# A three-branch transformer block and a two-layer block: the side work of the first three branches set out anew

## The chip, the cores and the metric

One Trainium2 chip, one of its cores. The metric is the device time of one execution in microseconds (us). Before the change the median of 3 runs is 2276.05 us (2275.41 to 2276.76).

## What the reference computes

512 tokens of width 1024 go through a first block with three mixers side by side and then through a second block of two layers. The change touches the three mixers of the first block alone.

```
h = rmsnorm(x);  proj = h @ w_in      # q,k,v of A; q,f,i,g of B; c_q,c_kv,c_kr of C; gate logits
y_a = chunked_relpos_attention(a_q, a_k, a_v, rel_bias)     # 8 heads of 64, softmax
y_b = hgrn2_recurrence(b_q, b_f, b_i, b_g, ...)             # q -> silu(q); k = sigmoid(-f)
                                                            # gated by silu(g)
y_c = mla_attention(c_q, c_kv, c_kr, ...)                   # rmsnorm of c_q and c_kv first
merged = sum over n of sigmoid(gate_n) * (y_n @ w_branch[n])
x = x + merged @ w_out;  x = x + relu(h2 @ w_ff1)^2 @ w_ff2
```

All is in 32-bit floats. Each dense product is made of three matmuls with operands split in a high part (rounded to the fp32r type) and a low part: high by low, high by high, low by high.

## The kernel before, in words

A planner (class `Plan`) writes one list of steps. Each engine's program walks the same list in order and emits its own part of a step, so the list sets the order on every engine, and each engine runs its queue strictly in that order. Semaphores carry the dependences. Nothing is reordered on the chip by due time or cost.

The dense products are the backbone. A "unit" is one weight tile's product. A `rows` unit has 128 output columns and eight 128-deep steps; it is issued in four pieces of six matmuls. A `cols` unit has 512 columns for four token blocks, in 16 pieces of six matmuls, and takes its weights in four chunks. Weights come by DMA into two buffers `raw`; ACT copies a chunk to its high part (`split`, L1321) and DVE makes the low part in the following piece (`split_low`, through `low`, L1642). The last piece of a unit or chunk is followed by the split of the chunk two further on, and by the step `ev`, which empties the unit's PSUM bank.

With some units a "side" generator is interleaved: `interleave(main, side, ratio)` places `ratio` side ticks behind each dense piece on average, so now and then two in a row. Beside the units `uB` (query and output-gate inputs of mixer B, 8 units, 32 pieces) runs attention A, 39 ticks; beside `uGA` (gates and projection of A, 48 pieces) runs the recurrence of B; beside `uGB` runs mixer C (`mla`). Between them stand `uF` (the values, then the forget gates of B; one `cols` unit each) and `uC` (latents of C).

In a tick n of attention A, PE computes scores n and n+1 (even n, L1009), transposes the weights of item n-4 into bank 6 (L910), and DVE adds the bias, takes the maximum of item n-1 and normalises item n-2. ACT exponentiates item n-1 (L1445), then copies the transposed item n-4 out of bank 6 (`turned`, L1462). Bank 6 is the only bank for these transposes, so the transpose of one item waits for the copy of the item before.

A logistic 1/(1+exp(-z)) is three ACT instructions on a 128x512 tile: Exp, Ln, Exp (L1417, L1419, L1421), each waiting for the one before. For `bq`, `bg` and `gate` units they stand back to back in `ev`, after DVE has scaled the bank (`scale`, L1757). For `bq` and `bg` the step `ev2`, one piece later, lets DVE multiply the bank by the logistic (L1860, L1862) and so frees the bank (2 or 3, in turn).

The forget gates (`bf`) are four steps of DVE and ACT on four token blocks (L1873, L1880, L1883 on DVE; L1428, L1430, L1434 on ACT), after which PE turns the keys (`h_turn`). The latent norm is one step `c_norm`: ACT squares four blocks and takes their roots, then DVE scales them in eight instructions (L2046, L2047); PE turns them in `c_turn`.

Of the kernel before, what the change touches and what calls it, by code (L numbers as in the profile page):

```python
# [8 lines left out]
ACT = mybir.ActivationFunctionType  # L9
# [158 lines left out]
def cols(w, c0, ncol, src, ev, **arg):  # L168
    return Unit("cols", w, 0, 8, c0, ncol, src, ev, **arg)
# [84 lines left out]
class Plan:  # L254
# [57 lines left out]
    def ready(self, u, j):  # L312

        steps = (self.split(u.chunks[0] + 2) if j == u.n - 1 else []) + [("ev", u, j)]
        if u.ev == "out" and u.arg["norm"] is not None:
            self.defer(1, "ev_low", u, j)
        if u.ev == "up" and u.arg["n"] == 2:
            self.defer(2 if u.arg["m"] < 4 else 1000, "merge", u.arg["m"] + j)
        if u.arg.get("ship"):
            self.defer(2, "ship", u, j)  # L320
        if u.ev in ("bq", "bg"):
            self.defer(1, "ev2", u)
        return steps

    def heads(self, u):
# [60 lines left out]

    def hgrn(self):

        for _ in range(7):
            yield []  # L390
        for p in range(4):
            yield [("h_turn", p)]
        for tt in range(4):
            yield [("h_decay", tt)]
        exps = [(p, lv) for p in range(4) for lv in (1, 2, 3, 7, 4, 5, 6)]
        ends = []
        yield [("h_zero",), ("h_exp", *exps.pop(0))]
        yield [("h_weigh", 0, 1), ("h_exp", *exps.pop(0))]
        weigh = [(0, 2)]
        for p in range(4):  # L400
            for lv in range(8):
                tick = [("h_weigh", *w) for w in weigh]
                weigh = []
                if ends:
                    tick.append(ends.pop(0))
                if lv < 7:
                    tick.append(("h_score", p, lv))
                    if lv == 2:
                        tick.append(("h_state", p))
# [12 lines left out]

    def mla(self):

        def steps(g):
            return [[(n, g, i)] for n in ("c_q", "c_kv", "c_qt", "c_kt") for i in range(4)]

        for _ in range(7):
            yield []
        for j in range(3):  # L430
            yield [("c_turn", j)]
        yield [("c_rope",)]
        yield from steps(0)
# [20 lines left out]
    def make(self):  # L454
        win, win2a, win2b = ("w_in", 0), ("w_in_2", 0), ("w_in_2", 1)
        h0, h1 = ("h", 0), ("merged", 1)
# [2 lines left out]
        uA += [cols(win, 1024, 512, h0, "vcopy", to="F3")]  # L459
        uB = [rows(win, 0, 8, 1536 + j * P, P, h0, "bq", j=j, wk=4 + j) for j in range(4)]  # L460
        uB += [rows(win, 0, 8, 3072 + j * P, P, h0, "bg", j=j, wk=4 + j) for j in range(4)]
        uF = [cols(win, 2560, 512, h0, "vcopy", to="F0"), cols(win, 2048, 512, h0, "bf")]
        uGA = self.gate_up(0, "yA")
        uC = [cols(win, 3584, 416, h0, "c")]
        uGB = self.gate_up(1, "yB")
# [71 lines left out]
        self.banks = (0, 1, 6, 7)  # L537
        self.run(self.dense(uA[8:]))
        self.banks = (2, 3)
        self.run(interleave(self.dense(uB), self.attn(ATTN["A"]), 39 / 32))  # L540
        uF[0].banks, uF[1].banks = [0, 1, 4, 5], [2, 3, 6, 7]
        self.run(self.dense(uF))
        self.banks = (0, 1)
        recurrence = list(self.hgrn())
        self.run(interleave(self.dense(uGA, {i: [("bf", uF[1], i)] for i in range(4)}), iter(recurrence[:-4]), 49 / 48, False))
        self.banks = (0, 1, 4, 5)
        self.run(self.dense(uC, {2 + 2 * i: t for i, t in enumerate(recurrence[-4:])}))
        self.add("c_norm")
# [348 lines left out]
def tensor_program(pe, S, B, plan):  # L897
# [226 lines left out]
    def h_state(p):  # L1124
        two = [empty(b) for b in h_pair(p, 7)]
        at.wait_ge("hg_dk", 4)
        for tt in range(4):
            at.wait_ge(*plan.freed(plan.uF[0], tt)[0])
        k4, v4 = B.f4("F1"), B.f4("F0")
        for c in range(7):  # L1130
            rr, cs = slice(64 * (c % 2), 64 * (c % 2) + 64), slice((c // 2) * 64, (c // 2) * 64 + 64)
            for hf in range(2):
                hs = slice(p * P + 64 * hf, p * P + 64 * hf + 64)
                last = pe.matmul(two[c % 2][64 * hf:64 * hf + 64, cs], k4[rr, c // 2, hs], v4[rr, c // 2, hs],
                                 start=c < 2, stop=True, skip_group_check=True)
# [162 lines left out]
def scalar_program(act, S, B, plan, load_table):  # L1298
# [106 lines left out]
    def sigmoid(u):  # L1405
        bank = B.bank[u.banks[0]]
        if u.ev == "gate":
            w = B.W[u.arg["at"] % 4]
            bank = w
        else:  # L1410
            w = B.W[u.arg["wk"]]
            if "before" in u.arg:
                at.wait_ge("ev_d", u.arg["before"].dve[0])
                if u.ev == "fgate":
                    at.wait_ge("f_lo", u.arg["before"].arg["tile"] + 1)
        at.wait_ge("ev_s", u.scaled[0])
        act.activation(w[:], bank[:], ACT.Exp, scale=-1.0).then_inc(S["ev_a"], 1)  # L1417
        at.wait_ge("ev_a", u.act[0])
        act.activation(w[:], w[:], ACT.Ln, bias=one).then_inc(S["sig"], 1)  # L1419
        at.wait_ge("sig", u.sig - 1)  # L1420
        act.activation(w[:], w[:], ACT.Exp, scale=-1.0).then_inc(S["sig"], 1)  # L1421

    def bf(u, i):
        k = B.f4("F1")
# [10 lines left out]


    def attn(a, n):
        i = n - a.e
        if 0 <= i < a.nt:
            nk, w, st = (a.where(i)[1] + 1) * P, B.W[a.P1[i % 4]], B.stat(i)  # L1440
            src = w if a.name == "A" else B.bank[a.X[i % len(a.X)]]
            if i >= 4:
                at.wait_ge("at_t", a.i(i - 4))
            at.wait_ge("at_m", a.i(i))
            act.activation(w[:, 0:nk], src[:, 0:nk], ACT.Exp, bias=st[:, 0:1],  # L1445
                           accum_out=st[:, 1:2]).then_inc(S["at_e"], 1)
        if 0 <= n - a.t < a.nt:
            turned(a, n - a.t)
        p = a.ends(n - a.o - 1)
        if p is not None:  # L1450
            y = a.pair(p) - 1
            ys = slice(y % 4 * T, (y % 4 + 1) * T)
            at.wait_ge("at_o", y + 1)
            act.copy(B.R[0][:, ys], B.bank[7][:]).then_inc(S["at_yh"], 1)
# [80 lines left out]
        act.copy(B.R[2][:, p * T:(p + 1) * T], B.V(3)).then_inc(S["yb_h"], 1)  # L1535


    def c_norm():
        at.wait_ge("hg_s", 28)
        for tt in range(4):  # L1540
            o, w, s = B.c_tokens()[:, tt, :], B.W[4 + tt], B.stat(tt)
            at.wait_ge(*plan.freed(plan.uC[0], tt)[0])
            act.activation(w[:, 0:256], o[:, 0:256], ACT.Square, accum_out=s[:, 0:1]).then_inc(S["c_n"], 1)
            act.activation(w[:, 256:384], o[:, 256:384], ACT.Square, accum_out=s[:, 1:2]).then_inc(S["c_n"], 1)
        s = B.st[:, 0:32].rearrange("p (t c) -> p t c", t=4)
        at.wait_ge("c_n", 8)
        act.activation(s[:, :, 2:3], s[:, :, 0:1], ACT.Ln, bias=eps, scale=1.0 / 256).then_inc(S["c_n"], 1)
        act.activation(s[:, :, 3:4], s[:, :, 1:2], ACT.Ln, bias=eps, scale=1.0 / 128).then_inc(S["c_n"], 1)
        at.wait_ge("c_n", 10)
        act.activation(s[:, :, 2:4], s[:, :, 2:4], ACT.Exp, scale=-0.5).then_inc(S["c_n"], 1)  # L1550
# [67 lines left out]
    def dt(u, h):  # L1618
# [3 lines left out]
        act.mul(B.F[u.arg["to"]][:, h * T:(h + 1) * T], B.bank[6][:], gain).then_inc(S["dt_a"], 1)  # L1622

    todo = {"begin": begin, "late": late, "split": split, "first": first, "root": root, "root2": root2, "merge": merge, "at": attn, "df": diff, "df_soft": diff_soft, "df_norm": diff_norm,
            "ev": ev, "ev_low": ev_low, "bf": bf,
            "h_decay": h_decay, "h_exp": h_exp, "h_sq": h_sq, "h_ms": h_ms, "h_low": h_low, "c_norm": c_norm, "c_q": c_q,
            "c_qt": c_qt, "c_kv": c_kv, "c_kt": c_kt, "sb": sb, "dn_sq": dn_sq, "dn_root": dn_root, "dt": dt}
    for step in plan.steps:
        if step[0] in todo:
# [6 lines left out]
def vector_program(dve, S, B, plan):  # L1636
# [402 lines left out]
        low(B.R[3][:, ps], B.V(3), B.R[2][:, ps], "yb_l")  # L2039


    def c_norm():
        for tt in range(4):
            o, s = B.F["F4"][:, tt * 416:(tt + 1) * 416], B.stat(tt)
            at.wait_ge("c_n", 11)
            dve.tensor_scalar(o[:, 0:256], o[:, 0:256], s[:, 2:3], None, ALU.mult).then_inc(S["c_u"], 1)  # L2046
# [406 lines left out]
```

## Time and profile before

| | value |
|---|---|
| median of 3 runs | 2276.05 us |
| the profiled execution | 2277.32 us, span 2275.6 us |
| granted TensorE clock, mean | 0.996 of full speed |
| PE busy | 2220.9 us (98%) |
| DVE, ACT, POOL busy | 1200.1, 940.3, 219.6 us |
| chain of waits, shares | PE 89%, DVE 4%, ACT 4%, issue 2% |

PE's busy time leaves 54.7 us of the span. The page's 40 slices show where: PE stands at 8 tenths in the first slice and at 9 in all others. Where an idle time of PE is shown in the timeline, the engine named behind the arrow is the one whose instruction ended it.

### The profile page before, as it was taken

Reading aid. Unit: us, or ns where it says so; the run is one execution under the profiler, and the core shown is the slowest. Engines: PE = TensorE matmul, PEld = TensorE weight load, DVE = VectorE, ACT = ScalarE, POOL = GpSimd, SP = SyncE. Lnnn points to the kernel's source line nnn. Section 1 sums busy time; section 2 is a strip of 40 time slices with the busy share of each in tenths; the row PEclk is TensorE's granted clock in tenths of the full one; section 3 lists DMA queues with packets and bytes.
Section 4 is the critical chain, followed back from the end, with each engine's and each line's share of the span. In section 5 each row is a group of like instructions: output and inputs, shape, how many; then the busy total and the mean of one; then the engine's idle time right before and its main releaser. Section 6 shows DMA issues by size and latency. Waiting matters only on the chain.

```text
span 2275.6 us, 26925 instructions
## 1 busy us (share of the span) xinstructions
PE 2220.9 (98%) x10484; PEld 1733.9 (76%) x10484; DVE 1200.1 (53%) x1827; ACT 940.3 (41%) x1561; POOL 219.6 (10%) x312
## 2 busy tenths in 40 slices
PE   8989999999999999999999999999999999999999
PEld 6658788667888888877565788888887657888887
DVE  4573664555544444473445555545545685555454
ACT  4463433455443223243545533333435565333331
POOL 0000121211210000030323200000120001000000
PEclk9999999999999999999999999999999999999999
DMA  5212111212323222322011232222321112332233
GB/s 171 74 42 88 47 37 63 68 38 102 102 93 100 96 96 98 102 84 93 29 56 38 74 102 93 95 100 93 102 93 65 56 47 68 101 101 92 93 102 102
DMA packets 52111, 187.48 MB, mean 82 GB/s; under 512 B 5905, under 2 KB 6033, under 8 KB 51857
## 3 DMA queue, kind: packets, MB, share of 16 engines
q1 hardware_dynamic: 51984, 185.76, 24.6%
q8 instruction: 84, 1.38, 0.3%
q14 instruction: 43, 0.34, 0.1%
HBM read 183.64 MB, written 2.10 MB: 82 GB/s over the span
## 4 chain that ended last, share of the span: by engine, by line
PE 89%; DVE 4%; ACT 4%; issue 2%; POOL 1%; DMA 1%; SPq 0%; ACTq 0%; DVEq 0%; POOLq 0%
PE ps L925 22%; PE ps L928 21%; PE ps L926 21%; PE ps L946 4%; PE ps L949 3%; PE ps L947 3%; PE ps L1269 2%; PE ps L910 2%; PE ps L1120 1%; PE ps L1153 1%; PE ps L1257 1%; PE ps L1245 1%; ACT wh L1321 1%; PE ps L1273 1%; PE ps L1033 1%
## 5 line engine op out<-in xcount | busy, mean ns | idle before, releaser
L1321 ACT CAST wh<-raw 128x1024 fp32r<-128x1024 f32 (+1 forms) x336 | 353.0, 1051 | 874.1 <-PE ps L928 758.3
L925 PE MATMUL ps<-hh,wl 128*128 128x512 f32 x1408 | 566.9, 403 | 14.6 <-DVE wl L1642 13.2
L928 PE MATMUL ps<-hl,wh 128*128 128x512 f32 x1408 | 551.2, 391 | 0.0
L926 PE MATMUL ps<-hh,wh 128*128 128x512 f32 x1408 | 550.4, 391 | 0.0
L1642 DVE TENSOR_TENSOR wl<-raw,wh 128x1024 fp32r<-128x1024 f32 (+1 forms) x336 | 416.4, 1239 | 191.5 <-ACT wh L1321 190.4
L925 PE MATMUL ps<-R,wl 128*128 128x512 f32 x896 | 359.5, 401 | 7.3 <-issue 5.8
L928 PE MATMUL ps<-R,wh 128*128 128x512 f32 x896 | 350.6, 391 | 0.0
L926 PE MATMUL ps<-R,wh 128*128 128x512 f32 x896 | 350.1, 391 | 0.0
L925 PEld LDWEIGHTS ps<-hh,wl 128*128 128x128 f32 x1408 | 265.7, 189 | 73.3 <-issue 20.4
L928 PEld LDWEIGHTS ps<-hl,wh 128*128 128x128 f32 x1408 | 265.4, 188 | 56.9 <-DVE hl L1721 0.3
L926 PEld LDWEIGHTS ps<-hh,wh 128*128 128x128 f32 x1408 | 265.8, 189 | 55.9 <-issue 2.9
L1852 DVE TENSOR_TENSOR x<-ps,x 128x512 f32<-128x512 f32 x192 | 131.6, 689 | 143.2 <-PE ps L928 143.2
L925 PEld LDWEIGHTS ps<-R,wl 128*128 128x128 f32 x896 | 169.1, 189 | 46.6 <-issue 11.1
L928 PEld LDWEIGHTS ps<-R,wh 128*128 128x128 f32 x896 | 168.9, 188 | 36.2 <-DVE R L1642 0.4
L926 PEld LDWEIGHTS ps<-R,wh 128*128 128x128 f32 x896 | 168.9, 189 | 35.2 <-issue 1.4
L946 PE MATMUL ps<-wh,hh 128*128 128x512 f32 (+1 forms) x384 | 155.4, 405 | 1.0 <-ACT F L1376 0.5
L949 PE MATMUL ps<-wh,hl 128*128 128x512 f32 (+1 forms) x384 | 148.9, 388 | 0.0
L947 PE MATMUL ps<-wl,hh 128*128 128x512 f32 (+1 forms) x384 | 148.7, 387 | 0.0
L2161 POOL TENSOR_TENSOR W<-W 128x512 f32<-128x512 f32 x30 | 48.6, 1620 | 837.8 <-ACT W L1340 837.1
L1757 DVE TENSOR_TENSOR ps<-ps,W 128x512 f32<-128x512 f32 x96 | 67.2, 700 | 114.3 <-PE ps L928 114.3
L1642 DVE TENSOR_TENSOR R<-W,R 128x512 fp32r<-128x512 f32 x84 | 58.2, 693 | 87.4 <-ACT R L1403 78.7
L946 PEld LDWEIGHTS ps<-wh,hh 128*128 128x128 f32 x384 | 72.3, 188 | 23.7 <-issue 9.7
(225 smaller groups left out, 2195.5 us busy)
## 6 DMA issues: line engine op xcount, KB each, us to landing
raw<-in_weights SPq DMA_DIRECT2D x332, 512.0 KB, 3.3
x<-in_x_t SPq DMA_DIRECT2D x4, 512.0 KB, 7.2
F<-in_x_t SPq DMA_DIRECT2D x4, 512.0 KB, 4.6
out<-x SPq DMA_DIRECT2D x8, 256.0 KB, 2.1
raw<-in_weights SPq DMA_DIRECT2D x4, 416.0 KB, 3.1
x<-in_bias SPq DMA_DIRECT2D x1, 1024.0 KB, 6.2
C<-in_consts SPq DMA_DIRECT2D x1, 832.0 KB, 6.8
F<-in_weights SPq DMA_DIRECT2D x2, 384.0 KB, 3.6
```

The source lines that it names most:

```text
L910: last = pe.transpose(bank[0:rows, i * P:(i + 1) * P], a, ident)
L925: pe.matmul(out, lo[:, k, cs], xh, start=k == 0, stop=False)
L926: pe.matmul(out, hi[:, k, cs], xh, start=False, stop=False)
L928: last = pe.matmul(out, hi[:, k, cs], xl, start=False, stop=k == u.nk - 1)
L946: pe.matmul(out, B.hh[:, ts], hi[:, kk, :], start=k == 0, stop=False)
L947: pe.matmul(out, B.hh[:, ts], lo[:, kk, :], start=False, stop=False)
L949: last = pe.matmul(out, B.hl[:, ts], hi[:, kk, :], start=False, stop=k == 7)
L1321: act.copy(B.wh[s][:, 0:nk * ncol], B.raw[s][:, 0:nk * ncol]).then_inc(S["w_hi"], 1)
L1642: dve.tensor_tensor(lo, src, hi.bitcast(F32), ALU.subtract).then_inc(S[name], 1)
L1757: dve.tensor_tensor(to[:], B.bank[u.banks[j]][:], B.W[8][:], ALU.mult).then_inc(S["ev_s"], 1)
L1852: dve.tensor_tensor(B.xt(m), bank[:], before, ALU.add).then_inc(S["ev_d"], 1)
L2161: pool.tensor_tensor(B.W[0][:], B.W[0][:], B.W[m][:], ALU.add).then_inc(S["n_addp"], 1)
```

## The change

Five things are moved; no arithmetic is added or left out.

- In attention A ACT's copy `turned` stands ahead of the exponential of the same tick.
- The second and third instruction of a logistic become steps of their own (`sig2`, `sig3`), one and two pieces after `ev`, for `bq`, `bg` and `gate`; `ev2` stands three pieces after instead of one. For the feed-forward gates (`fgate`) the three stay together.
- The unit of the forget gates comes ahead of the values. Attention A's 39 ticks are spread over 36 pieces (32 of `uB`, 4 of the forget gates) instead of 32. The four `bf` steps stand beside the values' pieces instead of `uGA`'s first ones.
- The recurrence begins after 2 empty ticks instead of 7, with 44 ticks to 48 pieces instead of 49.
- The latent norm's DVE scalings become two side ticks and its ACT part five, inside `mla`, in place of seven empty ticks.

```diff
@@ ready
+        if u.ev in ("bq", "bg", "gate"):
+            self.defer(1, "sig2", u)
+            self.defer(2, "sig3", u)
         if u.ev in ("bq", "bg"):
-            self.defer(1, "ev2", u)
+            self.defer(3, "ev2", u)
@@ hgrn
-        for _ in range(7):
+        for _ in range(2):
             yield []
@@ mla
-        for _ in range(7):
-            yield []
+        for tt in range(4):
+            yield [("c_sq", tt)]
+        yield [("c_root",)]
+        for i in range(2):
+            yield [("c_norm", i)]
@@ make
-        uF = [cols(win, 2560, 512, h0, "vcopy", to="F0"), cols(win, 2048, 512, h0, "bf")]
+        uF = [cols(win, 2048, 512, h0, "bf"), cols(win, 2560, 512, h0, "vcopy", to="F0")]
...
-        self.run(interleave(self.dense(uB), self.attn(ATTN["A"]), 39 / 32))
         uF[0].banks, uF[1].banks = [0, 1, 4, 5], [2, 3, 6, 7]
-        self.run(self.dense(uF))
+        made = list(self.dense(uB + uF, {49 + 3 * i: [("bf", uF[0], i)] for i in range(4)}))
+        self.run(interleave(iter(made[:36]), self.attn(ATTN["A"]), 39 / 36))
+        self.run(made[36:])
...
-        self.run(interleave(self.dense(uGA, {i: [("bf", uF[1], i)] for i in range(4)}), iter(recurrence[:-4]), 49 / 48, False))
+        self.run(interleave(self.dense(uGA), iter(recurrence[:-4]), 44 / 48, False))
...
-        self.add("c_norm")
@@ scalar_program: sigmoid
         act.activation(w[:], bank[:], ACT.Exp, scale=-1.0).then_inc(S["ev_a"], 1)
+        if u.ev == "fgate":
+            sig2(u)
+            sig3(u)
+    def sig2(u):
         at.wait_ge("ev_a", u.act[0])
-        act.activation(w[:], w[:], ACT.Ln, bias=one).then_inc(S["sig"], 1)
+        act.activation(sig_tile(u)[:], sig_tile(u)[:], ACT.Ln, bias=one).then_inc(S["sig"], 1)
+    def sig3(u):
         at.wait_ge("sig", u.sig - 1)
-        act.activation(w[:], w[:], ACT.Exp, scale=-1.0).then_inc(S["sig"], 1)
+        act.activation(sig_tile(u)[:], sig_tile(u)[:], ACT.Exp, scale=-1.0).then_inc(S["sig"], 1)
@@ scalar_program: attn
+        if a.name == "A" and 0 <= n - a.t < a.nt:
+            turned(a, n - a.t)
         i = n - a.e
...
-        if 0 <= n - a.t < a.nt:
+        if a.name != "A" and 0 <= n - a.t < a.nt:
             turned(a, n - a.t)
```

ACT's queue in attention A, around the second `bq` unit: W5 is that unit's logistic, W0 to W3 the attention items, F7, F5, F8 the transposed items' places, wh the high weights. Before:

```order
L1462 COPY F7<-ps 128x3x128
L1321 CAST wh1<-raw1 128x1024
L1417 ACTIVATE W5<-ps 128x512
L1419 ACTIVATE W5<-W5,C 128x512
L1421 ACTIVATE W5<-W5 128x512
L1445 ACTIVATE W0,st<-W0,st 128x128
L1462 COPY F5<-ps 128x3x128
L1445 ACTIVATE W1,st<-W1,st 128x128
L1462 COPY F7<-ps 128x4x128
L1445 ACTIVATE W2,st<-W2,st 128x256
L1462 COPY F5<-ps 128x4x128
```

After:

```order
L1463 ACTIVATE W2,st<-W2,st 128x512
L1327 CAST wh1<-raw1 128x1024
L1423 ACTIVATE W5<-ps 128x512
L1480 COPY F7<-ps 128x3x128
L1463 ACTIVATE W3,st<-W3,st 128x512
L1433 ACTIVATE W5<-W5,C 128x512
L1480 COPY F5<-ps 128x3x128
L1463 ACTIVATE W0,st<-W0,st 128x128
L1437 ACTIVATE W5<-W5 128x512
L1480 COPY F7<-ps 128x4x128
L1463 ACTIVATE W1,st<-W1,st 128x128
L1480 COPY F5<-ps 128x4x128
```

Between two copies to F7 and F5 there stood the high weights, three logistic instructions and an exponential; now each stretch between two copies holds an exponential and one part of that.

DVE's queue at the latent norm: F4 are the latents, wl the low weights, W0 and W1 the scaled gates. Before:

```order
L1788 TENSOR_SCALAR F4<-ps,st 128x416 x2
L2046 TENSOR_SCALAR F4<-F4,st 128x256
L2047 TENSOR_SCALAR F4<-F4,st 128x128
L2046 TENSOR_SCALAR F4<-F4,st 128x256
L2047 TENSOR_SCALAR F4<-F4,st 128x128
L2046 TENSOR_SCALAR F4<-F4,st 128x256
L2047 TENSOR_SCALAR F4<-F4,st 128x128
L2046 TENSOR_SCALAR F4<-F4,st 128x256
L2047 TENSOR_SCALAR F4<-F4,st 128x128
L1642 TENSOR_TENSOR wl1<-raw1,wh1 128x1024
L1757 TENSOR_TENSOR W0<-ps,W8 128x512
L1642 TENSOR_TENSOR wl0<-raw0,wh0 128x1024
```

After:

```order
L1807 TENSOR_SCALAR F4<-ps,st 128x416 x2
L1661 TENSOR_TENSOR wl1<-raw1,wh1 128x1024
L2065 TENSOR_SCALAR F4<-F4,st 128x256
L2066 TENSOR_SCALAR F4<-F4,st 128x128
L2065 TENSOR_SCALAR F4<-F4,st 128x256
L2066 TENSOR_SCALAR F4<-F4,st 128x128
L1776 TENSOR_TENSOR W0<-ps,W8 128x512
L2065 TENSOR_SCALAR F4<-F4,st 128x256
L2066 TENSOR_SCALAR F4<-F4,st 128x128
L2065 TENSOR_SCALAR F4<-F4,st 128x256
L2066 TENSOR_SCALAR F4<-F4,st 128x128
L1661 TENSOR_TENSOR wl0<-raw0,wh0 128x1024
```

The low weights that stood behind all eight scalings stand ahead of them, and the gate's scaling stands between the fourth and the fifth.

DVE's queue behind the forget gates: F8 and F1 are the log gates and the keys (the last pair stands at the start), F0 the values, F2 the turned keys, W0 and W1 the first scaled gates. Before:

```order
L1880 SCALAR_TENSOR_TENSOR F8<-ps,st,W7 128x512
L1883 SCALAR_TENSOR_TENSOR F1<-ps,st,F8 128x512
L1757 TENSOR_TENSOR W0<-ps,W8 128x512
L1642 TENSOR_TENSOR wl0<-raw0,wh0 128x1024
L1757 TENSOR_TENSOR W1<-ps,W8 128x512
L1969 COPY F2<-ps 128x512
L1642 TENSOR_TENSOR wl1<-raw1,wh1 128x1024
L1969 COPY F2<-ps 128x512
L1841 TENSOR_TENSOR x<-ps,W0 128x512
L1969 COPY F2<-ps 128x512 x2
L1841 TENSOR_TENSOR x<-ps,W1 128x512
```

After:

```order
L1899 SCALAR_TENSOR_TENSOR F8<-ps,st,W7 128x512
L1902 SCALAR_TENSOR_TENSOR F1<-ps,st,F8 128x512
L1661 TENSOR_TENSOR wl0<-raw0,wh0 128x1024
L1802 TENSOR_SCALAR F0<-ps,st 128x512 x2
L1661 TENSOR_TENSOR wl1<-raw1,wh1 128x1024
L1776 TENSOR_TENSOR W0<-ps,W8 128x512
L1988 COPY F2<-ps 128x512
L1661 TENSOR_TENSOR wl0<-raw0,wh0 128x1024
L1988 COPY F2<-ps 128x512 x3
L1776 TENSOR_TENSOR W1<-ps,W8 128x512
L1994 TENSOR_TENSOR F1<-F1,F7 128x512
```

Between the last keys and the first gate's scaling now stand two low weights and the values' evacuation; before, that scaling and the first low weights of `uGA`'s stretch came right behind the keys.

## Rows read from the trace of the kernel before

**Rows 1.** Page part 1: engines' busy us, share of span, instructions.
```profile
PE 2220.9 (98%) x10484; PEld 1733.9 (76%) x10484; DVE 1200.1 (53%) x1827; ACT 940.3 (41%) x1561; POOL 219.6 (10%) x312
```

**Rows 2.** Stretches: start:end, length; each engine's busy us; PEclk, DMA share, GB/s.
```profile
91.50:175.70 84.20, 72.86 (x359) 46.11 (x357) 61.50 (x156) 50.03 (x121) 0.00 (x0) 0.96 0.15 44
232.00:260.00 28.00, 24.65 (x120) 18.67 (x121) 14.29 (x20) 13.40 (x20) 3.07 (x2) 0.94 0.24 76
402.00:440.00 38.00, 37.48 (x166) 28.27 (x167) 16.89 (x33) 15.72 (x30) 11.07 (x18) 0.96 0.27 87
440.00:520.00 80.00, 74.64 (x362) 52.59 (x361) 46.63 (x127) 44.07 (x109) 11.84 (x20) 1.00 0.12 40
```

**Rows 3.** Waits of PE, 90 to 200 us: total us, times, longest.
```profile
PE ps L910 <- ACT F L1462: 11.3, 11, 2.0
```

**Rows 4.** Timeline of PE, attention stage: start us, us, line, operation [idle before].
```profile
97.03 0.48 PE L925 MATMUL ps<-hh,wl 128*128 128x512 f32 x1
...
97.81 0.39 PE L925 MATMUL ps<-hh,wl 128*128 128x512 f32 x1
...
98.49 0.38 PE L910 MATMUL ps<-C,W 128*128 128x128 f32 x2
...
146.08 0.55 PE L910 MATMUL ps<-C,W 128*128 128x128 f32 x3 [2.00 <-ACT F L1462]
```

**Rows 5.** Timeline of ACT, same stage.
```profile
141.99 1.05 ACT L1321 CAST wh<-raw 128x1024 fp32r<-128x1024 f32 x1
142.94 0.59 ACT L1417 ACTIVATE W<-ps 128x512 f32<-128x512 f32 x1
143.57 0.72 ACT L1419 ACTIVATE W<-W,C 128x512 f32<-128x512 f32 x1
144.32 0.63 ACT L1421 ACTIVATE W<-W 128x512 f32<-128x512 f32 x1
...
145.56 0.46 ACT L1462 COPY F<-ps 128x384 f32<-128x384 f32 x1
```

**Rows 6.** Waits of DVE, 91.5 to 175.7 us.
```profile
DVE F L1862 <- ACT W L1421: 1.4, 2, 0.7
```

**Rows 7.** Timeline of PE, 230 to 258 us.
```profile
232.54 0.63 PE L910 MATMUL ps<-C,F 128*128 128x128 f32 x4 [0.84 <-ACT F L1434]
234.69 0.47 PE L925 MATMUL ps<-R,wl 128*128 128x512 f32 x1 [1.52 <-issue]
...
255.94 1.16 PE L1120 MATMUL ps<-C,F 128*128 128x128 f32 x8 [1.29 <-ACT F L1519]
```

**Rows 8.** Timeline of DVE, 230 to 236 us.
```profile
233.36 1.22 DVE L1642 TENSOR_TENSOR wl<-raw,wh 128x1024 fp32r<-128x1024 f32 x1 [1.03 <-ACT wh L1321]
```

**Rows 9.** Timeline at 394 to 403 us: ACT, then DVE, then PE.
```profile
394.50 1.04 ACT L1321 CAST wh<-raw 128x1024 fp32r<-128x1024 f32 x1
...
399.12 0.35 DVE L2046 TENSOR_SCALAR F<-F,st 128x256 f32<-128x256 f32 x1 [5.04 <-ACT st L1550]
...
400.96 1.22 DVE L1642 TENSOR_TENSOR wl<-raw,wh 128x1024 fp32r<-128x1024 f32 x1
402.09 0.68 DVE L1757 TENSOR_TENSOR W<-ps,W 128x512 f32<-128x512 f32 x1
...
402.32 0.47 PE L925 MATMUL ps<-hh,wl 128*128 128x512 f32 x1 [2.93 <-DVE wl L1642]
```

**Rows 10.** Timeline at 369 to 372 us: DVE, then PE.
```profile
369.74 1.29 DVE L2024 COPY_PREDICATED F<-C,ps 128x256 f32<-128x256 uint32 x2 [0.35 <-PE ps L1153]
...
371.18 1.14 PE L1167 MATMUL ps<-F 128*64 128x128 f32 x16 [1.55 <-DVE F L2024]
```

**Rows 11.** Timeline at 489 to 492 us: ACT, then PE.
```profile
489.30 0.63 ACT L1417 ACTIVATE W<-W 128x512 f32<-128x512 f32 x1 [0.71 <-DVE W L1757]
...
491.25 0.56 ACT L1565 COPY F<-ps 96x512 f32<-96x512 f32 x1
...
491.87 0.64 PE L910 MATMUL ps<-C,F 128*96 128x128 f32 x4 [1.67 <-ACT F L1565]
```

More of the change, by code:

```diff
@@ L1127, in h_state @@
         for tt in range(4):
-            at.wait_ge(*plan.freed(plan.uF[0], tt)[0])
+            at.wait_ge(*plan.freed(plan.uF[1], tt)[0])
         k4, v4 = B.f4("F1"), B.f4("F0")
@@ L1417, in sigmoid, with sig_tile @@
         act.activation(w[:], bank[:], ACT.Exp, scale=-1.0).then_inc(S["ev_a"], 1)
+        if u.ev == "fgate":
+            sig2(u)
+            sig3(u)
+    def sig_tile(u):
+        return B.W[u.arg["at"] % 4 if u.ev == "gate" else u.arg["wk"]]
+    def sig2(u):
         at.wait_ge("ev_a", u.act[0])
-        act.activation(w[:], w[:], ACT.Ln, bias=one).then_inc(S["sig"], 1)
+        act.activation(sig_tile(u)[:], sig_tile(u)[:], ACT.Ln, bias=one).then_inc(S["sig"], 1)
+    def sig3(u):
         at.wait_ge("sig", u.sig - 1)
-        act.activation(w[:], w[:], ACT.Exp, scale=-1.0).then_inc(S["sig"], 1)
+        act.activation(sig_tile(u)[:], sig_tile(u)[:], ACT.Exp, scale=-1.0).then_inc(S["sig"], 1)
     def bf(u, i):
@@ L1535, in h_low, with c_sq, c_root @@
         act.copy(B.R[2][:, p * T:(p + 1) * T], B.V(3)).then_inc(S["yb_h"], 1)
-    def c_norm():
+    def c_sq(tt):
+        o, w, s = B.c_tokens()[:, tt, :], B.W[4 + tt], B.stat(tt)
         at.wait_ge("hg_s", 28)
[L1540 to L1544, printed above, removed]
+        at.wait_ge(*plan.freed(plan.uC[0], tt)[0])
+        act.activation(w[:, 0:256], o[:, 0:256], ACT.Square, accum_out=s[:, 0:1]).then_inc(S["c_n"], 1)
+        act.activation(w[:, 256:384], o[:, 256:384], ACT.Square, accum_out=s[:, 1:2]).then_inc(S["c_n"], 1)
+    def c_root():
         s = B.st[:, 0:32].rearrange("p (t c) -> p t c", t=4)
@@ L1624, in scalar_program @@
     todo = {"begin": begin, "late": late, "split": split, "first": first, "root": root, "root2": root2, "merge": merge, "at": attn, "df": diff, "df_soft": diff_soft, "df_norm": diff_norm,
-            "ev": ev, "ev_low": ev_low, "bf": bf,
-            "h_decay": h_decay, "h_exp": h_exp, "h_sq": h_sq, "h_ms": h_ms, "h_low": h_low, "c_norm": c_norm, "c_q": c_q,
+            "ev": ev, "ev_low": ev_low, "sig2": sig2, "sig3": sig3, "bf": bf,
+            "h_decay": h_decay, "h_exp": h_exp, "h_sq": h_sq, "h_ms": h_ms, "h_low": h_low, "c_sq": c_sq, "c_root": c_root, "c_q": c_q,
             "c_qt": c_qt, "c_kv": c_kv, "c_kt": c_kt, "sb": sb, "dn_sq": dn_sq, "dn_root": dn_root, "dt": dt}
@@ L2039, in h_low, with c_norm @@
         low(B.R[3][:, ps], B.V(3), B.R[2][:, ps], "yb_l")
-    def c_norm():
-        for tt in range(4):
+    def c_norm(i):
+        for tt in (2 * i, 2 * i + 1):
             o, s = B.F["F4"][:, tt * 416:(tt + 1) * 416], B.stat(tt)
```

## Prediction, on record before the changed kernel was run

> **What bounds the kernel now.** I read the page's busy times first: PE works 98% of the span [rows 1], so a change that leaves its work alone can win only PE's idle time and the stretches at the lower of its two clocks. The next view is the timeline of PE with its idle times. The feed-forward parts, from about 600 us on, have next to none. The change reaches the stretch up to 600 us. The stretches [rows 2] give both prices by stage: length less PE busy is idle time, and (1 - granted clock) times length is what the 1.2 GHz level took from work that would have run at 2.4 GHz.
>
> - Attention A: one wait makes up all: the transpose L910 waits for ACT's copy L1462, 11.3 us in 11 waits [rows 3]. The granted clock of 0.96 over 84.2 us is another 0.04 x 84.2 = 3.4 us [rows 2]. Together 14.7 us.
> - Start of `uGA` and of the recurrence: 0.84 + 1.52 + 1.29 = 3.65 us of waits [rows 7], and 0.06 x 28 = 1.7 us of clock [rows 2].
> - First pieces of `uGB`: a wait of 2.93 us [rows 9], and 0.04 x 38 = 1.5 us of clock [rows 2].
> - End of the recurrence: 1.55 us [rows 10].
> - Mixer C: 80 - 74.64 = 5.4 us idle between 440 and 520 us, at the full clock [rows 2].
>
> That is 31 us in reach. The rest of PE's idle time (10 us at the start, waiting for the first weights, and a few waits in the second block) isn't touched.
>
> **Attention A.** ACT's queue at the longest wait [rows 5]: weights 1.05 us, the logistic 0.59, 0.72 and 0.63, an exponential, and at 145.56 the copy, 3.6 us after the weights began. PE stood until 146.08, 2.00 us [rows 4]. In the new queue weights and one logistic part stand before the same copy, and neither the other two parts (0.72 + 0.63 us) nor the exponential: the copy starts at about 141.99 + 1.0 + 0.6 = 143.6 and ends at 144.1, which is when PE came to stand (146.08 - 2.00). So this wait goes to about nothing. The shorter ones have the same cause with less in it: an exponential that waits for DVE's maximum no longer stands ahead of the copy.
>
> What is late next. First, two ticks in a row with nothing between them: the second transpose must wait for the copy of the first, 0.46 us [rows 5] and about 0.1 us of signalling. The old ratio has seven such pairs, the new one three, and of these one stands where neither scores nor a product cover the copy: 0.6 us. Second, DVE. It is busy 61.5 of 84.2 us [rows 2]. Without PE's waits and clock loss, and with four pieces more (1.4 us each), the same stretch would be 84.2 - 14.7 + 5.6 = 75.1 us, so DVE would be at 82%, and above 90% where the items are 384 and 512 wide. Its scaling of the bank comes later then, and the first logistic part that waits for it holds up a copy. I take 0.3 us for each of eight units, 2.4 us. Left: 3.0 of 11.3 us; gain 8.3. By bounds this residue lies between 0.6 us (DVE never late) and 6.5 us (half the old waits and the pair). The clock fell behind waits like the one of 2.00 us; with none near that I expect all 3.4 us back.
>
> The new `ev2` has to be finished before the second unit after it starts, and it now stands two pieces later. A unit with its ticks is about 9.1 us long: four pieces of 1.46 and 4.3 ticks of 0.75 (69.5 us without waits and clock loss, less some 30 pieces, over some 35 ticks). `ev2` is reached after three pieces and their ticks, about 7 us, and takes 0.7. Two waits of DVE for the last logistic part, up to 0.7 us each, go at the same time [rows 6]. So PE's margin is about 1.5 us; I take no cost.
>
> A price: a dense piece next to single-precision side work is slower. The first matmul behind it takes 0.48 us against 0.39 [rows 4], and such a piece 98.49 - 97.03 = 1.46 us. With the lead-in of scores I take 0.15 us a piece, for four more pieces in A and five more beside the recurrence: +1.4 us (0.8 to 2.0).
>
> **Forget gates ahead of the values.** Their DVE and ACT work, whose end PE awaited at 232.54, and the low weights at 233.36 that were late because the high weights queued behind it [rows 7, 8], now lie beside 16 pieces of the values (22 us). The chain there is two splits of weights (1.05 + 1.22 us each) and sixteen instructions a side of 0.6 to 0.75 us, an estimate of 13 us to the last keys; weights keep about 1 us of margin a chunk. The third wait stands behind a whole logistic, which is now in three parts. All 3.65 us go, and with them the clock's 1.7 us: 5.35. From below, if the values' weights are late once, 1.5 us less.
>
> **Latent norm.** The low weights stood behind the eight scalings: these began at 399.12, when ACT had the roots, and the low weights at 400.96, although their high part was done at 395.54 [rows 9]. Now they stand ahead and are ready at about 397, before PE needs them at 402.32 - 2.93 = 399.4. What is late next is the first `c_turn`, which waits for all eight scalings. Four from 399.12 to 400.04, the gate's scaling 0.68 [rows 9], four more: 401.7. PE gets there one piece later, at 400.8: 0.9 us, say 1.0. Gain 1.9 us, with the clock 1.5: 3.4. Bounds: 1.0 (clock stays low, scalings late) to 4.4.
>
> **End of the recurrence.** The last product waited for DVE's last copies, 1.29 us, because two ticks stood together [rows 10]. At 44 ticks to 48 pieces there is a piece of 1.4 us between them. Gain 1.4 us (0.5 to 1.55).
>
> **Mixer C.** Its copies keep their place; the logistic parts go apart. The wait of 1.67 us ended with a copy that stood behind all three parts; behind one part it would start at 489.30 + 0.6 = 489.9 instead of 491.25 [rows 11], so 1.4 us go. Of the other 3.7 us most wait for exponentials that wait for DVE; I take 0.6. Gain 2.0 us (0 to 4).
>
> **Sum.** 8.3 + 3.4 + 5.35 + 3.4 + 1.4 + 2.0 - 1.4 = 22.45 us. From the profiled execution's 2277.32 us that gives 2254.9; it lies 1.3 us above the median of the runs, so from 2276.05: 2253.6 us.
>
> **A rule weighed.** The clock's part of the sum is 3.4 + 1.7 + 1.5 = 6.6 us, all from stretches behind waits that go [rows 2]. The Trainium skill ("TensorE: Matmul & The Clock Gate", "A second HAM failure mode: psum-queue depth-cycling") holds that frequent short idles between groups of matmuls are enough to make the clock go down and up again. The trace of before speaks against it: 440 to 520 us has 5.4 us of idle in short waits and a clock of 1.00 [rows 2]. By the trace 6.6 us come back; by the rule none need.
>
> **Rivals.**
> 1. DVE leads attention A. For it: its 82%. Against: before, no wait of PE there was ended by DVE [rows 3]. Then 6.5 us of waits stay instead of 3.0, and the clock's 3.4 us stay too: 2253.6 + 3.5 + 3.4 = 2260.5.
> 2. The clock stays as it is, since many short waits remain in all three stages: 2253.6 + 6.6 = 2260.2. Against it is the stretch of mixer C. The rule of the Trainium skill weighed above would have it so.
> 3. The change doesn't do what it says: the copies still queue behind weights and first logistic part in A, and mixer C doesn't move; 8.3 + 3.4 + 2.0 fall away: 2267.3. Against: the queue position at 141.99 to 145.56.
> 4. Slower: the later `ev2` becomes the wait. If DVE is so late that the bank is free 1.9 us after PE wants it, for each of eight units, and each such wait brings a clock loss of 1.7 us like that of [rows 2], it costs 8 x 3.6 = 28.8 us, and the kernel stands at 2253.6 + 28.8 = 2282.4. It decides from 2.8 us a unit on. Against: DVE still had 84.2 - 61.5 = 22.7 us of idle time in the stretch [rows 2], and nothing in it made PE wait for DVE [rows 3].
>
> **Chances.** Forecast with its own range of 2249 to 2258: 0.62. DVE 0.17, clock 0.08, change without effect in A 0.07, slower 0.03, and 0.03 for something between the last two. The range for eight in ten is 2248 to 2264: below it all residues at their lower bound (2.4 us in A, 1.0 at the latent norm, 2.0 in mixer C, 0.6 of the changeovers: 6.0 less, so 2247.6), above it rivals 1 and 2 with the latent norm's lower bound. About 0.2% (4.6 us) is what can be told from no change; that line is at 2271.5. Faster 0.94, same 0.03, slower 0.03.
>
> **What would show it.** In attention A the sum of L910's waits for the copy should be 2 to 4 us instead of 11.3 and the clock 1.00. No wait at the first turned keys and none for weights behind them. The first weights of `uGB` without a wait, and about 1 us at the first `c_turn`. No wait at the last product of the recurrence. If instead PE's first matmul of a `bq` or `bg` unit waits for DVE's product with the logistic, the fourth rival is right; if L910 waits for DVE's normalised weights, the first.

## The result and the profile after

The changed kernel takes 2243.31 us (median of 4 runs, 2242.92 to 2243.97); the kernel before, run beside it, 2275.73. The ratio is 0.9861, 95% interval 0.9844 to 0.9878. The profiled execution took 2243.45 us with a span of 2241.7. The forecast was 2253.6 with a range of 2248 to 2264: the direction was right and the gain, 22.4 us by forecast, was 32.4. The time lies 4.7 us below the range.

The page's busy times and granted clock (tenths of full speed, 40 slices), of after, answer to [rows 1]:

```profile
PE 2209.7 (99%) x10484; PEld 1728.2 (77%) x10484; DVE 1202.2 (54%) x1827; ACT 935.6 (42%) x1561; POOL 219.7 (10%) x312
...
PE   8999999999999999999999999999999999999999
...
PEclk9999999999999999999999999999999999999999
```

PE is busy 11.2 us less with the same matmuls, mostly since the stretches at the lower clock are gone: those of [rows 2] and two more told of below. What is left of it is at the very start in both kernels: there a matmul takes 0.63 us instead of 0.39 until 16 us. The mean granted clock is 1.00. PE's row of before is

```profile
PE   8989999999999999999999999999999999999999
```

so not only the first slice stood at 8 tenths but the third too, 114 to 171 us, which is attention A. It is that slice that has filled up.

The list of all that PE waited for (engine, line, who ended it; us in total, times, longest), of after:

```profile
PE ps L931 <- DVE wl L1661: 10.8, 2, 10.6
...
PE ps L1209 <- ACT W L1463: 1.4, 1, 1.4
...
PE ps L916 <- DVE F L2066: 1.0, 1, 1.0
PE ps L916 <- ACT F L1480: 0.7, 1, 0.7
```

The transpose's wait for the copy, which was 11.3 us in 11 waits [rows 3], is one of 0.7 us (L916 and L1480 are L910 and L1462 of before). The first row is the start of the program, as before. The waits of [rows 7], [rows 10] and the 2.93 us of [rows 9] are gone from the list; what is late next at the latent norm is the first turn, 1.03 us, which the prediction worked out as 0.9 and rounded to 1.0.

To see where the time went I cut both traces at the same matmul: a dense step is a triple of matmuls, and the start of the first one of `uB`, `uGA`, `uC`, `uGB` and `uGC` is the same work in every kernel. All lengths are in us; "waits" is PE's idle time in the stage, and "forecast" is what the prediction's terms give for it.

| stage | before | waits | after | waits | gain | forecast |
|---|---|---|---|---|---|---|
| `uB` + `uF` (attention A, forget gates) | 137.33 | 11.34 | 122.12 | 0.74 | 15.2 | 11.1 |
| `uGA` (recurrence) | 153.28 | 5.20 | 145.19 | 0.00 | 8.1 | 6.0 |
| `uC` | 19.85 | 0.00 | 19.12 | 0.00 | 0.7 | 0 |
| `uGB` (latent norm, mixer C) | 140.92 | 9.45 | 131.59 | 2.64 | 9.3 | 5.4 |
| `uGC` | 65.28 | 0.00 | 65.28 | 0.00 | 0.0 | 0 |

33.3 us in all, of which the start of the first stage, 83.85 us after and 83.33 before, takes 0.5 back. From the start of `uGB` on PE's order is the same in both kernels. In the profiled executions the gain is 33.9 us (2277.32 to 2243.45); 0.9 us of it lies in the second block and is told of at the end. Between the medians it is 32.4.

The stretches behind three of these lines (start:end, length; busy of PE, PEld, DVE, ACT, POOL; clock, DMA share, GB/s), before:

```profile
220.66:373.94 153.28, 148.08 (x1280) 118.88 (x1278) 94.44 (x171) 61.32 (x93) 33.40 (x24) 0.98 0.14 42
393.79:534.71 140.92, 131.48 (x621) 94.50 (x621) 74.78 (x187) 74.55 (x180) 26.13 (x45) 0.99 0.17 57
```

and after:

```profile
84.01:158.59 74.58, 73.84 (x377) 49.32 (x376) 64.23 (x167) 50.11 (x125) 0.00 (x0) 1.00 0.19 57
205.97:351.16 145.19, 145.19 (x1279) 117.06 (x1278) 89.22 (x160) 53.63 (x82) 33.49 (x24) 1.00 0.15 46
370.28:501.87 131.59, 128.94 (x622) 93.50 (x621) 75.00 (x187) 73.26 (x180) 26.92 (x45) 1.00 0.18 61
```

DVE is busy 64.23 of 74.58 us in attention A, 86% where [rows 2] had 73%, and PE waited for it nowhere in that stage.

### The profile page after: what moved, and what is told of

Same layout as the page of the kernel before. It is cut to its first block, busy times and chain, and to the rows that moved or that the text cites. A ratio compares the mean times of both kernels' runs of the same rounds, so it can differ in the third digit from the quotient of the medians.

```text
span 2241.7 us, 26926 instructions
## 1 busy us (share of the span) xinstructions
PE 2209.7 (99%) x10484; PEld 1728.2 (77%) x10484; DVE 1202.2 (54%) x1827; ACT 935.6 (42%) x1561; POOL 219.7 (10%) x312
## 3 DMA queue, kind: packets, MB, share of 16 engines
q8 instruction: 84, 1.38, 0.3%
## 4 chain that ended last, share of the span: by engine, by line
PE 93%; DVE 2%; ACT 2%; issue 1%; POOL 1%; DMA 0%; POOLq 0%; SPq 0%; ACTq 0%; DVEq 0%
PE ps L931 23%; PE ps L934 22%; PE ps L932 22%; PE ps L952 4%; PE ps L955 4%; PE ps L953 3%; PE ps L916 2%; PE ps L1275 2%; PE ps L1126 1%; PE ps L1159 1%; PE ps L1015 1%; PE ps L1263 1%; PE ps L1251 1%; PE ps L1279 1%; PE ps L1039 1%
```

## The experiments

The same cut by stage was made in the trace of each of them. The first four are the kernel before with one edit, the next four the changed kernel with one part undone, the last ones variants of it. "..." marks what is left out of an edit, such as the program text that goes with a step.

**One edit at a time.** The edits are those of the diff, alone on the kernel before.

s1_copies:

```diff
+        if a.name == "A" and 0 <= n - a.t < a.nt:
+            turned(a, n - a.t)
...
-        if 0 <= n - a.t < a.nt:
+        if a.name != "A" and 0 <= n - a.t < a.nt:
```

> The kernel before with one edit: in attention A ACT's copy out of bank 6 stands ahead of the tick's exponential. Theory 'each queue neighbour counts' (the exponential and the logistic each cause part of the waits): PE's waits for the copy fall from 11.3 us to 5 to 7 and the clock's 3.4 us come back in part; 2267 to 2270 us against 2275.7. Rival 'the logistic alone': the copy still stands behind three logistic parts where it mattered, waits stay above 9 us; 2273 to 2276.

Measured: 2270.57 us, ratio 0.9979 (0.9969 to 0.9989). PE's waits in attention A:

```profile
PE ps L910 <- ACT F L1464: 7.7, 10, 2.0
```

7.7 us are left of 11.3 and the stage (`uB` + `uF`) is 5.0 us shorter. Up to 1.7 us of that is clock: one of the stage's two stretches at the lower clock is gone. Both numbers lie between the two theories' bounds, so neither is shown by this run.

s2_logistic:

```diff
+        if u.ev in ("bq", "bg", "gate"):
+            self.defer(1, "sig2", u)
+            self.defer(2, "sig3", u)
         if u.ev in ("bq", "bg"):
-            self.defer(1, "ev2", u)
+            self.defer(3, "ev2", u)
...
```

> The kernel before with one edit: second and third logistic instruction one and two pieces later for bq, bg and gate units, the product ev2 three pieces later. Theory 'each queue neighbour counts': A gains 4 to 6 us, the start of the recurrence 1.3, mixer C 5 to 6 (all its waits but the one of 1.36 us); 2262 to 2266 us. Rival 'mixer C was cleared by the latent norm's new place upstream': mixer C gains under 2; 2268 to 2271.

Measured: 2261.64 us, ratio 0.9939 (0.9924 to 0.9954). Attention A is 6.0 us shorter, the recurrence 2.2, `uC` 0.7, and `uGB` 5.8. PE's waits in `uGB`:

```profile
PE ps L928 <- DVE wl L1655: 2.9, 1, 2.9
PE ps L1206 <- ACT W L1458: 1.4, 1, 1.4
PE ps L913 <- ACT F L1578: 0.2, 1, 0.2
```

Of mixer C's 6.5 us only one wait of 1.4 and one of 0.2 stand; the 2.9 us are the latent norm's. So the logistic parts alone make all of mixer C's gain, and the rival falls. Not all of the 14.4 us is theirs, though: at the end of the recurrence the wait of 1.6 us is still there, but in this execution no stretch at the lower clock came behind it. That is the 0.7 us in `uC`, where PE waits in neither kernel, and 0.9 of the 2.2.

s3_forget:

```diff
-        uF = [cols(win, 2560, 512, h0, "vcopy", to="F0"), cols(win, 2048, 512, h0, "bf")]
+        uF = [cols(win, 2048, 512, h0, "bf"), cols(win, 2560, 512, h0, "vcopy", to="F0")]
...
+        self.run(interleave(iter(made[:36]), self.attn(ATTN["A"]), 39 / 36))
...
```

> The kernel before with one edit: forget gates' unit ahead of the values, their steps beside the values, attention A over 36 pieces, recurrence after 2 empty ticks at 44 to 48. Theory: A gains 3 to 5 us by the thinner side work (seven pairs of ticks become three), the forget gates 5, the end of the recurrence 2.5 with its clock; 2263 to 2266 us. Rival 'thinning does nothing as long as the queue order is the old one': A gains under 1; 2268.

Measured: 2260.70 us, ratio 0.9936 (0.9921 to 0.9951), better than forecast. `uB` and `uF` are 8.3 us shorter and the recurrence 7.3. Attention A still waits, in the old queue order:

```profile
PE ps L911 <- ACT F L1463: 5.8, 5, 2.2
```

11.3 us have become 5.8 by thinner side work alone (6.5 with one more in `uF`), so that rival falls as well. The clock of the stage is 1.00.

s4_latent:

```diff
-        for _ in range(7):
-            yield []
+        for tt in range(4):
+            yield [("c_sq", tt)]
+        yield [("c_root",)]
+        for i in range(2):
+            yield [("c_norm", i)]
...
-        self.add("c_norm")
...
```

> The kernel before with one edit: the latent norm as side ticks. Theory: the wait of 2.93 us for the low weights goes with the clock loss behind it, the first turn of the latents waits 1 us; mixer C unchanged; 3.6 us less, 2272 us. Rival 'it also clears mixer C': 7 us less or more, 2268.

Measured: 2272.57 us, ratio 0.9988 (0.9979 to 0.9998). `uGB` is 3.5 us shorter, where the prediction had 3.4 and the expectation 3.6, and mixer C's waits are as before.

By stage the four gains add in `uGB` (5.8 + 3.5 = 9.3, together 9.3) but not in attention A: 5.0 + 6.0 + 8.3 = 19.3 against 15.2. Much of that overlap of 4.1 us is the clock. The granted clock was 0.96 before and is 0.98, 0.98 and 1.00 with the three edits, so each alone already takes one or both of the same two stretches at the lower clock.

**One part undone.** Each of these is the changed kernel with one of the same edits taken back.

m1_no_copies:

```diff
-        if a.name == "A" and 0 <= n - a.t < a.nt:
-            turned(a, n - a.t)
...
```

> The changed kernel with ACT's copy behind the exponential again. By itself the copy's place was worth 5.0 us in attention A. If the edits add, the stage is 5 us longer than the changed one and the kernel 2248 us. If they are substitutes (the logistic already out of the way, the ticks thinner), it is under 2.5 us longer; 2244 to 2246. The sum of the four single gains (38.8 us) is above the joint one (32.4), so I expect the substitutes here: 2 us, 2245.3.

Measured: 2246.36 us, ratio to the kernel before 0.9876 (0.9861 to 0.9891). `uB` + `uF` 124.86 against 122.12 us, waits of 2.4 us instead of 0.7. The copy's place is worth 2.7 us here and 5.0 alone: the edits are substitutes, a little less so than expected (2 us).

m2_no_logistic:

```diff
-            self.defer(1, "sig2", u)
-            self.defer(2, "sig3", u)
-            self.defer(3, "ev2", u)
+            self.defer(1, "ev2", u)
...
```

> The changed kernel with each logistic in one piece and its product one piece later, as before. Mixer C loses the 5.8 us it gained by this edit alone. In attention A it gained 6.0 alone; if substitutes, 2 to 4 here. At the recurrence under 1. 2252 to 2254 us; if all adds, 2257.

Measured: 2255.55 us, ratio to the kernel before 0.9917 (0.9900 to 0.9933), the dearest part to undo. `uGB` loses 5.8 us, as by itself; attention A 5.3 (127.44), nearly the 6.0 it gained alone, and not 2 to 4. So the time lies above the 2252 to 2254 us expected, and in attention A the logistic and the other edits are hardly substitutes.

m3_no_forget:

```diff
-        self.run(interleave(iter(made[:36]), self.attn(ATTN["A"]), 39 / 36))
+        self.run(interleave(self.dense(uB), self.attn(ATTN["A"]), 39 / 32))
...
-        self.run(interleave(self.dense(uGA), iter(recurrence[:-4]), 44 / 48, False))
+        self.run(interleave(self.dense(uGA, {i: [("bf", uF[1], i)] for i in range(4)}), iter(recurrence[:-4]), 49 / 48, False))
...
```

> The changed kernel with the old order of values and forget gates, 39 ticks to 32 pieces, seven empty ticks and 49 to 48. The recurrence's stage loses 5 to 7 us (two of its old waits come from the logistic). Attention A at the old density with copies ahead and logistic apart: if DVE's load is what bounds it then, 4 us or more of waits come back; if the queue order was all, under 2. I expect 3 in A and 6 in the recurrence: 2252 to 2253 us.

Measured: 2253.11 us, ratio to the kernel before 0.9906 (0.9891 to 0.9920). Attention A and `uF` take 126.36 us (4.2 more), the recurrence 149.70 (4.5 more, where 5 to 7 were expected). Three of the old waits are back there, 0.8, 1.5 and 1.6 us; the fourth, of 1.29, belonged to the logistic. But the clock stays at 1.00 behind the three, where before it fell twice behind the same waits.

m6_ratio32:

```diff
-        self.run(interleave(iter(made[:36]), self.attn(ATTN["A"]), 39 / 36))
+        self.run(interleave(iter(made[:32]), self.attn(ATTN["A"]), 39 / 32))
```

> The changed kernel with attention A beside the 32 pieces of uB alone at 39 to 32, all else as changed. Separates the thinner side work from the new order of the forget gates. Theory 'density matters': 2 to 4 us of waits in A, 2246 to 2247 us. Rival 'with the queue in this order density is free': within 1 us of the changed kernel.

Measured: 2247.81 us, ratio to the kernel before 0.9882 (0.9867 to 0.9896). PE's waits for the copy (total, times, longest):

```profile
PE ps L916 <- ACT F L1480: 3.8, 6, 1.1
```

`uB` + `uF` take 126.35 us, as in m3_no_forget, so all of that stage's loss there is the density. It is 4.2 us more than in the changed kernel, of which only 3.8 - 0.7 = 3.1 are waits: the other 1.1 us are in no row of waits. What they are is told below, under what a wait costs.

**Variants.**

v1_ev2_4:

```diff
-            self.defer(3, "ev2", u)
+            self.defer(4, "ev2", u)
```

> The changed kernel with the product ev2 four pieces after its unit instead of three. By the prediction's own margin of 1.5 us, with a piece and its tick at 2.3 us, the bank would come 0.8 us late for each of eight units: 6 us of new waits of PE on DVE's product at the first matmul of bq and bg units. Rival 'DVE runs a piece ahead of PE, so the margin is larger': under 1 us in all.

Measured: 2248.03 us, ratio to the kernel before 0.9875 (0.9857 to 0.9893). The timeline of PE (start, length, line, operation, [idle before]):

```profile
100.43 0.47 PE L931 MATMUL ps<-hh,wl 128*128 128x512 f32 x1 [1.33 <-DVE F L1881]
...
109.54 0.47 PE L931 MATMUL ps<-hh,wl 128*128 128x512 f32 x1 [0.45 <-DVE F L1881]
...
122.62 0.47 PE L931 MATMUL ps<-hh,wl 128*128 128x512 f32 x1 [1.03 <-DVE F L1881]
...
143.26 0.47 PE L931 MATMUL ps<-hh,wl 128*128 128x512 f32 x1 [1.03 <-DVE F L1879]
```

Four of eight banks come late, by 0.5 to 1.3 us, and `uB` + `uF` are 4.4 us longer (126.50; 6 us of waits were expected). The latest came 1.33 us late after one piece and its ticks (2.3 us) more, so at three pieces the margin there was about 1.0 us, of 1.5 forecast. The fourth rival was one piece away.

v2_scale_first:

```diff
-        for i in range(2):
-            yield [("c_norm", i)]
+        yield [("c_norm", 0), ("c_norm", 1)]
+        yield []
```

> The changed kernel with all eight scalings of the latent norm in one tick, so that the first gate's scaling stands behind them. Theory: the wait of 1.03 us at the first turn of the latents goes (they are done 1.6 us earlier) and no other comes; 1.0 us less in that stage. Rival: the gate's scaling is late then and the wait moves to the gate's bank; no gain.

Measured: 2243.18 us, ratio to the kernel before 0.9854 (0.9838 to 0.9869). The wait at the first turn:

```profile
376.99 0.63 PE L916 MATMUL ps<-C,F 128*128 128x128 f32 x4 [0.43 <-DVE F L2066]
```

0.43 us instead of 1.03, and the stage is 0.55 us shorter; half of what was expected, as the scalings can't begin before the roots and only the gate's scaling of 0.69 us no longer stands among them. By its median this is the fastest kernel of the study, but its 0.1 us can't be told from the changed one by the runs.

v3_copies_all:

```diff
-        if a.name != "A" and 0 <= n - a.t < a.nt:
-            turned(a, n - a.t)
```

(and the first condition without the name A.)

> The changed kernel with the copy ahead of the exponential in mixer C too. There scores stay in PSUM until the exponential frees their bank, and two banks take the transposes. Theory: the exponential is what PE waits for there (1.36 us once), so the copy ahead makes it later: 0 to 2 us more in that stage. Rival 'copies first is good wherever there are transposes': 0.3 to 1.4 us less.

Measured: 2245.77 us, ratio to the kernel before 0.9865 (0.9848 to 0.9883). What PE waited for in `uGB` (total, times, longest):

```profile
PE ps L1209 <- ACT W L1463: 1.7, 1, 1.7
...
PE ps L1015 <- ACT W L1463: 0.6, 1, 0.6
PE ps L916 <- DVE W L1944: 0.6, 1, 0.6
```

The stage takes 133.52 us, 1.9 longer. The rival falls. In mixer C the exponential frees the scores' bank, so PE waits for it: the wait at L1209 is 1.7 us instead of 1.36, and two of 0.6 us are new.

v4_ratio40 (attention A over 40 pieces) was not run: the forget unit's piece 33 and the mask of attention item 31 would wait for each other. So 40 pieces stay untried.

v5_ratio38:

```diff
-        self.run(interleave(iter(made[:36]), self.attn(ATTN["A"]), 39 / 36))
+        self.run(interleave(iter(made[:38]), self.attn(ATTN["A"]), 39 / 38))
```

(with the edit of v2_scale_first.)

> All eight scalings of the latent norm in one tick, and attention A spread over 38 pieces at 39 to 38, so that the one pair of ticks left stands behind the last product. Theory 'each pair of ticks costs its wait and a hidden part': attention A's last wait (0.74 us) goes; A and the two units behind it together 0.7 to 1.0 us shorter than in the changed kernel, 2242.0 us in all. Rival 'each changeover between dense and single-precision work costs 0.15 us': two more changeovers, 0.4 us shorter only.

Measured: 2243.81 us, ratio to the kernel before 0.9866 (0.9849 to 0.9882). The timeline of PE:

```profile
159.22 0.50 PE L952 MATMUL ps<-wh,hh 128*128 128x512 f32 x1 [1.30 <-DVE W L1934]
```

The wait of 0.74 us is gone as forecast, but a new one of 1.30 stands where the forget unit's first matmul needs a score bank that DVE has yet to read. `uB` + `uF` are 122.75 us, 0.6 more than in the changed kernel; neither theory named this wait. Without it they are 121.45, against 122.12 - 0.74 = 121.38 at 36 pieces: two more changeovers, with two pairs of ticks fewer, come to 0.07 us.

## Why the prediction was right and where it was wrong

**What was right.** Each named wait went, for the reason given where an experiment could show it: the forget gates' and the weights' behind them (s3_forget), the low weights at the latent norm (s4_latent, 3.5 us against 3.4), and the copy's (s1, s2, s3 each take part of it). The first turn waits 1.03 us, forecast 1.0. The clock came back whole: `uGB` after has three waits and a clock of 1.00. So the second rival fell. The Trainium skill ("TensorE: Matmul & The Clock Gate", "A second HAM failure mode: psum-queue depth-cycling") tells of a kernel whose frequent short idles between groups of matmuls made the clock go down and up. Of that the traces here show a part: in before the clock fell behind waits as short as 1.55 us [rows 10], but 5.4 us of short ones between 440 and 520 us, one of them 1.67, left it at 1.00 [rows 2, 11]. DVE led nowhere, so the first rival fell, although DVE is busy 86% of attention A.

All the rivals stood for a smaller gain; the prediction named none for a larger one and gave it no chance of its own.

The profiled executions differ by 33.9 us, 11.4 more than the sum of 22.45. These are:

**Mixer C, 3.8 us: the step that failed.** Forecast 2.0, measured 5.8. The prediction said: "Of the other 3.7 us most wait for exponentials that wait for DVE; I take 0.6." It read the last arrow of a wait and took DVE for its cause. PE's waits in the stage before (total, times, longest) were, besides the latent norm's,

```profile
PE ps L910 <- ACT F L1565: 1.7, 1, 1.7
PE ps L1033 <- ACT F L1462: 1.4, 1, 1.4
PE ps L1203 <- ACT W L1445: 1.4, 1, 1.4
PE ps L1009 <- ACT W L1445: 1.1, 3, 0.7
PE ps L910 <- ACT F L1462: 1.0, 1, 1.0
```

The first was priced right: 1.4 us forecast, 1.42 measured. Of the others only the one of 1.36 at L1203 stayed. Those that went inside the stretch of 440 to 520 us gave 2.8 us and not 0.6. Two more, at 438.10 and 528.52 us, lie outside the stretch that the prediction had looked at and gave another 1.65. With mixer C's 3.8 us right, the same sum would have come to 2249.8, inside the range; the terms below took the time below it.

The chain of waits of before, from 509 us to the product's wait of 1.39 us at 515.86 (start, us, what), shows what stands behind DVE:

```profile
509.06 1.05 ACT wh L1321
510.11 0.54 ACT W L1417
...
510.67 0.73 ACT W L1419
...
511.43 0.63 ACT W L1421
512.06 0.36 ACT W L1445 x2
...
512.44 0.17 DVE st L1925
...
512.64 0.29 DVE W L1927
512.93 1.13 DVE wl L1642
...
514.06 0.12 DVE ps L1918
...
514.21 0.44 DVE st L1920
...
514.67 0.57 ACT W L1445 x2
515.24 0.48 ACT F L1462
...
515.86 2.16 PE ps L1033 x12
```

The weights and the three logistic parts (509.06 to 512.06) hold up an exponential; DVE's reciprocal waits for its sum, the low weights and the next maximum queue behind the reciprocal, the next exponential waits for that maximum, and the copy waits for the exponential. The lateness goes from ACT to DVE and back. In the changed kernel, with one logistic part there instead of three, ACT's rows are:

```profile
478.72 1.05 ACT L1327 CAST wh<-raw 128x1024 fp32r<-128x1024 f32 x1
479.67 0.63 ACT L1423 ACTIVATE W<-W 128x512 f32<-128x512 f32 x1
480.20 0.36 ACT L1463 ACTIVATE W<-ps,st 128x128 f32<-128x128 f32 x1
```

The exponential starts 1.5 us after the weights (478.72 to 480.20) and not 3.0, and PE doesn't wait for the product. s2_logistic shows that this edit alone does it, and m2_no_logistic that it is lost without it.

**The residue in attention A, 2.3 us.** Term "Left: 3.0 of 11.3 us", measured 0.74. The pair of ticks was right (0.6 forecast; the one wait is 0.74 us at 142.02, at the second of two transposes with no dense piece between). The 0.3 us a unit for a late DVE weren't there: the forecast read DVE's busy share as lateness. Why DVE was never late no run separates; that its steps stand ahead of what PE needs, with nothing left that holds them up, is a reading of the queues.

**The changeovers, 1.4 us.** 0.15 us for each further dense piece beside side work were charged, from one first matmul of 0.48 us instead of 0.39 [rows 4]. The longer row was there, but it was no loss. v5_ratio38 puts two more at 0.07 us. In the recurrence m3_no_forget has five fewer than the changed kernel and PE is busy 145.78 us there against 145.19, not less but more; the difference goes with its three waits, as told below.

**The rest, 3.9 us.** 0.9 are those of the second block. 1.7 are clock at the end of the recurrence, a term that the prediction put at nothing without a reason: it priced the wait of 1.55 us [rows 10] and did not look at the clock behind it. The stretches around it, of before (columns as above):

```profile
366.00:372.00 6.00, 4.45 (x54) 3.73 (x54) 4.14 (x6) 0.89 (x1) 0.87 (x1) 1.00 0.00 0
372.00:378.00 6.00, 6.00 (x52) 5.57 (x48) 0.00 (x0) 0.60 (x1) 0.00 (x0) 0.72 0.23 71
378.00:394.00 16.00, 16.00 (x83) 15.32 (x82) 6.55 (x8) 5.28 (x8) 0.00 (x0) 1.00 0.27 86
```

0.28 x 6.00 us is 1.7, half of it in `uGA` and half in `uC`, which is 0.7 us shorter after with no wait in it in either kernel. About 1 us is in attention A, in no row of waits; the ten waits that went are enough for it at the price below. The other 0.3 us is rounding and start.

**What a wait costs.** A wait costs more than its row. In `uGB`, matmul by matmul, the six waits that went (0.19, 0.27, 0.68, 1.67 less 0.25, 1.39, 0.96 us by their rows, 4.91 in all) moved the following matmul by 0.47, 0.53, 0.87, 1.42, 1.38 and 1.18, 5.85 us in all. PE's busy time in `uB` + `uF` shows the same. All these executions stand at a clock of 1.00 in that stage:

| run | pieces beside attention A | waits of PE | PE busy, us |
|---|---|---|---|
| after | 36 | 1 | 121.35 |
| v5_ratio38 | 38 | 1 | 121.45 |
| m2_no_logistic | 36 | 5 | 121.94 |
| m1_no_copies | 36 | 5 | 122.26 |
| v1_ev2_4 | 36 | 5 | 122.28 |
| s3_forget | 36 | 6 | 122.40 |
| m6_ratio32 | 32 | 6 | 122.54 |

It rises by 0.15 to 0.24 us with each further wait, also where the pieces, and with them the pairs of ticks, are the same. So most of the 1.1 us of m6_ratio32 that no row shows is the price of its five further waits. These numbers ask for no cost of ticks that stand together, nor for one of changeovers.

**Not settled:** what makes up these 0.2 us of a wait, whether a small cost of pairs of ticks is hidden beside it, and how attention A's gain splits among the three edits, which depends on the order in which they are made.

## What to carry to other kernels

When a wait ends on engine X, follow the chain back until it leaves the pair of engines that hand work to each other: a block of three instructions on one of them can be the cause of every "waits for the other" in the next few microseconds. In attention A, splitting such a block over the next ticks was worth 6.0 us and putting the urgent instruction first 5.0. Over the whole kernel it was 14.4 against 5.5, since the split also worked in mixer C, where putting the copy first cost 1.9 us (v3_copies_all). A high busy share of an engine is no wait: here 86% went without one. And an instruction whose result frees a buffer can be put off only up to its margin; one piece more cost 4.4 us.

## What the runs showed that was not expected

The clock did not fall behind every long wait. In before it fell behind one of 2.25 us; in after, at the same matmul of the second block and behind one of 2.24, it did not. PE's timeline there, before:

```profile
1896.87 0.47 PE L925 MATMUL ps<-R,wl 128*128 128x512 f32 x1 [2.25 <-issue]
```

and after:

```profile
1863.90 0.47 PE L931 MATMUL ps<-R,wl 128*128 128x512 f32 x1 [2.24 <-issue]
```

The 20 us around it (columns as in the stretches above), before:

```profile
1890.00:1910.00 20.00, 16.42 (x63) 12.80 (x64) 16.03 (x18) 10.78 (x16) 7.31 (x5) 0.91 0.21 68
```

and after:

```profile
1857.00:1877.00 20.00, 16.38 (x69) 12.67 (x70) 16.03 (x18) 10.79 (x16) 7.32 (x5) 1.00 0.22 66
```

The clock is 0.91 and 1.00, and the difference accounts for 0.9 us of the difference between the two profiled executions (1896.87 - 1863.90 = 32.97 us there, 33.9 at the end), which the change did not make. Of the fourteen profiled executions, all with this wait of 2.2 us, the clock fell behind it in eight. In s3_forget a wait of 2.21 us in attention A passed without a loss too, and so did the three old waits of the recurrence in m3_no_forget. So a clock term taken from one execution is a term that the next execution may not have.
